# An MLP up-projection whose last low part is summed in SBUF by an adding GpSimd DMA

## The reference

```
def sq_relu_mlp(h, w_up, w_down):
    return jnp.square(jax.nn.relu(h @ w_up)) @ w_down
...
x = x + sq_relu_mlp(rms_norm(x, mlp_norm_g[l]), w_up[l], w_down[l])
```

## Time and profile before

| what | value |
|---|---|
| median of 2 runs | 2017.7 us (2017.51 to 2017.88) |
| profiled execution | span 2017.5 us, equal to the lower of the runs' times |
| TensorE busy | 2008.2 us, clock 0.999 of full |
| VectorE, ScalarE, GpSimd busy | 1520.8, 980.1, 13.2 us |
| DMA moved | 381.98 MB, 189 GB/s in the mean |
| a load of 1 MB, issue to landing | 5.0 to 5.3 us in the median |

### The profile page before, as it was taken

One profiled execution on the slowest core, in us unless ns is written; L12 is line 12 of the kernel. 1 busy time (PEld: TensorE's weight loads), 2 busy tenths in 40 slices (PEclk: granted clock), 3 DMA queues, 4 the chain that ended last, 5 costly groups with the idle time before them and its releaser, 6 DMA issues.

```text
span 2017.5 us, 26213 instructions
## 1 busy us (share of the span) xinstructions
PE 2008.2 (100%) x9284; PEld 1680.1 (83%) x9284; DVE 1520.8 (75%) x2217; ACT 980.1 (49%) x1263; POOL 13.2 (1%) x21
## 2 busy tenths in 40 slices
PE   9999999999999999999999999999999999999998
PEld 7888888888888888888888998888888888888887
DVE  7789998887568558757888787888558757855875
ACT  6555555444344434434446665554444434444443
POOL 0000000000000000000000000000000000000000
PEclk9999999999999999999999999999999999999999
DMA  8655555655555655655565554565655555565563
GB/s 297 214 170 189 181 167 176 209 194 193 193 190 179 209 189 185 208 189 185 188 208 172 139 150 146 198 219 188 208 188 187 204 191 187 175 218 188 168 219 114
DMA packets 218034, 381.98 MB, mean 189 GB/s; under 512 B 15600, under 2 KB 40560, under 8 KB 217968
## 3 DMA queue, kind: packets, MB, share of 16 engines
q1 hardware_dynamic: 217104, 379.03, 56.9%
q10 hardware_dynamic: 864, 2.10, 0.3%
HBM read 379.00 MB, written 2.10 MB: 189 GB/s over the span
## 4 chain that ended last, share of the span: by engine, by line
PE 97%; issue 2%; DVE 0%; ACT 0%; POOL 0%; POOLq 0%; DVEq 0%; ACTq 0%
PE acc L473 29%; PE acc L475 29%; PE acc L474 29%; PE acc L493 2%; PE acc L494 2%; PE acc L495 2%; PE acc L749 1%; PE acc L750 1%; PE acc L751 1%; PE side L802 0%; PE side L792 0%; PE side L560 0%; DVE wlo L1365 0%; PE side L571 0%; PE side L775 0%
## 5 line engine op out<-in xcount | busy, mean ns | idle before, releaser
L1365 DVE TENSOR_TENSOR wlo<-raw,whi 128x1024 fp32r<-128x1024 f32 (+2 forms) x700 | 836.2, 1212 | 357.2 <-ACT whi L896 353.8
L896 ACT ACTIVATE whi<-raw 128x1024 fp32r<-128x1024 f32 (+2 forms) x700 | 726.3, 1050 | 708.2 <-PE acc L475 677.1
L473 PE MATMUL acc<-whi,opB 128*128 128x512 f32 x1296 | 505.5, 390 | 0.0
L475 PE MATMUL acc<-whi,opB 128*128 128x512 f32 x1296 | 504.4, 389 | 0.0
L474 PE MATMUL acc<-wlo,opB 128*128 128x512 f32 x1296 | 504.2, 389 | 0.0
L473 PE MATMUL acc<-whi,opA 128*128 128x512 f32 (+2 forms) x1296 | 501.8, 387 | 0.0
L475 PE MATMUL acc<-whi,opA 128*128 128x512 f32 (+2 forms) x1296 | 501.0, 387 | 0.0
L474 PE MATMUL acc<-wlo,opA 128*128 128x512 f32 (+2 forms) x1296 | 501.0, 387 | 0.0
L475 PEld LDWEIGHTS acc<-whi,opB 128*128 128x128 f32 x1296 | 243.2, 188 | 50.7
L473 PEld LDWEIGHTS acc<-whi,opB 128*128 128x128 f32 x1296 | 243.3, 188 | 50.4 <-DVE wlo L1365 0.3
L474 PEld LDWEIGHTS acc<-wlo,opB 128*128 128x128 f32 x1296 | 243.3, 188 | 50.1
(11 more groups left out here) (256 smaller groups left out, 1109.0 us busy)
## 6 DMA issues: line engine op xcount, KB each, us to landing
raw<-in_w_up SPq DMA_DIRECT2D x128, 1024.0 KB, 5.3
raw<-in_w_down SPq DMA_DIRECT2D x128, 1024.0 KB, 5.0
raw<-in_a_w_qkv SPq DMA_DIRECT2D x44, 1024.0 KB, 5.1
raw<-in_a_w_o SPq DMA_DIRECT2D x16, 1024.0 KB, 5.0
raw<-in_b_w_o SPq DMA_DIRECT2D x16, 1024.0 KB, 5.0
raw<-in_w_ukv SPq DMA_DIRECT2D x32, 256.0 KB, 4.3
raw<-in_w_dkv SPq DMA_DIRECT2D x4, 1024.0 KB, 5.1
raw<-in_b_w_dq SPq DMA_DIRECT2D x4, 768.0 KB, 4.7
```

Source lines behind the costliest of these rows:

```text
L473: mm(o, a_hi, w_hi, start=first and c == 0, stop=False)
L475: done = mm(o, a_lo, w_hi, start=False, stop=last and c == chunks - 1)
L896: done = fn(whi[:, place:place + ch, 0:n], raw[:, r, c0:c0 + ch, 0:n], ACT.Copy)
L1365: done = tt_(wlo[:, place:place + ch, 0:n], raw[:, r, c0:c0 + ch, 0:n], whi[:, place:place + ch, 0:n].bitcast(F32), ALU.subtract)
```

## The change

In the 32 up blocks, half 7's low part isn't computed by VectorE. ScalarE writes the high part as before and then the raw weights times -1, rounded to fp32r, into `wlo` (that is minus the high part). GpSimd then issues a DMA that reads the same 256 rows by 512 columns of `w_up` from HBM, 512 KB, for a second time and adds them to what stands in `wlo[:, 6:8, :]`. TensorE waits for this sum (`lo_summed`) before half 7. VectorE skips half 7 and counts it in advance with half 6; SP, which overwrites `raw`, waits for ScalarE's second copy (`neg_ready`) before quad 3 of the next block. For this, SP's loops over the quarters are written in another order of nesting, with the same loads in the same order.

```diff
@@ SP @@
-            def whole(b, w, col, row=0):
+            def whole(b, w, col, row=0, summed=None):
                 for r in range(4):
+                    if r == 3 and summed is not None:
+                        sp.wait_ge(neg_ready, summed)
                     quad(b, r, w[:, bass.ds(row + 4 * r, 4), bass.ds(col, NB)])
...
-                with sp.Fori(0, QUARTERS) as q:
+                def up(q, j):
+                    n = JB * QUARTERS * l + JB * q + j
+                    whole(B_MLP[l] + 2 * JB * q + j, W_UP[l], D * q + NB * j,
+                          summed=None if isinstance(n, int) and n == 0 else n)
+
+                def down(q):
                     with sp.Fori(0, JB) as j:
-                        whole(B_MLP[l] + 2 * JB * q + j, W_UP[l], D * q + NB * j)
+                        whole(B_MLP[l] + 2 * JB * q + JB + j, W_DOWN[l], NB * j, row=KC * q,
+                              summed=JB * QUARTERS * l + JB * q + JB)
...
@@ GpSimd @@
+            def up_lo(l):
+
+                for n in range(JB * QUARTERS):
+                    pool.wait_ge(neg_ready, JB * QUARTERS * l + n + 1)
+                    pool.dma_start(wlo[:, 6:8, :], W_UP[l][:, KC - 2:KC, NB * n:NB * n + NB],
+                                   accum_op=ALU.add).then_inc(lo_summed, 16)
+
             stream_scale(0)
             with pool.Fori(0, DA_PAIRS) as p:
                 sub_norm(p)
+            up_lo(0)
             stream_scale(2)
...
+            up_lo(1)
...
@@ TensorE @@
+                def lo_ready_last(n, also=None):
+                    def ready(hf):
+                        if also:
+                            also(hf)
+                        if hf == 7:
+                            pe.wait_ge(lo_summed, 16 * n + 16)
+                    return ready
...
@@ ScalarE, split @@
                 done.then_inc(hi_ready, 1)
+                if kind == "up" and hf == 7:
+                    fn(wlo[:, place:place + 2, :], raw[:, r, c0:c0 + 2, :], ACT.Copy, scale=-1.0).then_inc(neg_ready, 1)
...
@@ VectorE, split @@
                 c0, place = 2 * (hf % 2), 2 * (hf % 4)
+                if kind == "up" and hf == 7:
+                    return
                 dve.wait_ge(hi_ready, 8 * b + hf + 1)
...
-                done.then_inc(lo_ready, 1)
+                done.then_inc(lo_ready, 2 if kind == "up" and hf == 6 else 1)
```

More of the change, by code:

```diff
@@ L252, in trunk @@
         lo_ready = sem("lo_ready")
+        neg_ready = sem("neg_ready")
+        lo_summed = sem("lo_summed")
         pe_halves = sem("pe_halves")
@@ L371, in mlp @@
             def mlp(l):
-                with sp.Fori(0, QUARTERS) as q:
-                    with sp.Fori(0, JB) as j:
-                        whole(B_MLP[l] + 2 * JB * q + j, W_UP[l], D * q + NB * j)
+                def up(q, j):
[3 more added lines that the diff above has]
+                def down(q):
+                    with sp.Fori(0, JB) as j:
+                        whole(B_MLP[l] + 2 * JB * q + JB + j, W_DOWN[l], NB * j, row=KC * q,
+                              summed=JB * QUARTERS * l + JB * q + JB)
+                for j in range(JB):
+                    up(0, j)
+                with sp.Fori(0, QUARTERS - 1) as q:
+                    down(q)
                     with sp.Fori(0, JB) as j:
-                        whole(B_MLP[l] + 2 * JB * q + JB + j, W_DOWN[l], NB * j, row=KC * q)
+                        up(q + 1, j)
+                down(QUARTERS - 1)
             mlp(0)
@@ L684, in up @@
                         for k in range(2):
-                            block_tok(B_MLP[l] + 2 * JB * q + 2 * i + k, 1 - k, u[1 - k] + U_QUARTER * q + i, opA)
+                            block_tok(B_MLP[l] + 2 * JB * q + 2 * i + k, 1 - k, u[1 - k] + U_QUARTER * q + i, opA,
+                                      ready=lo_ready_last(JB * QUARTERS * l + JB * q + 2 * i + k))
+                def lo_ready_last(n, also=None):
[5 more added lines that the diff above has]
+                    return ready
                 def hidden_ready(q):
@@ L691, in mlp @@
                     s = (j + 1) % 2
-                    block_tok(B_MLP[l] + j, s, u[s] + j // 2, opA, ready=None if j else opA_ready(v_in))
+                    block_tok(B_MLP[l] + j, s, u[s] + j // 2, opA,
+                              ready=lo_ready_last(JB * QUARTERS * l + j, None if j else opA_ready(v_in)))
                 with pe.Fori(0, QUARTERS - 1) as q:
@@ L1160, in up @@
                     for j in range(JB):
-                        body(B_MLP[l] + 2 * JB * q + j, {6: lambda: hid_high(q, j - 1)} if j else first)
+                        body(B_MLP[l] + 2 * JB * q + j, {6: lambda: hid_high(q, j - 1)} if j else first,
+                             kind="up")
                         drain_up(q, j)
@@ L1800, in up @@
                     for j in range(JB):
-                        body(B_MLP[l] + 2 * JB * q + j, turned(q, j - 1) if j else first)
+                        body(B_MLP[l] + 2 * JB * q + j, turned(q, j - 1) if j else first, kind="up")
                         square_up(q, j)
```

## The result

The changed kernel takes 2250.3 us in the median (2249.2 to 2251.3, 2 runs) against 2017.7: 1.115 times as long, 95% interval 1.113 to 1.117, or 232.6 us more. The profiled execution has a span of 2247.1 us, 229.6 more than before.

What follows compares the result with a forecast made beforehand. TensorE bounds the kernel, busy 2008.2 of 2017.5 us. A transfer of 1.0 + 5.3 + 2.2 = 8.5 us exceeds windows of 4.0 us (26 blocks) and 6.0 us (6): +132 us, 2150 us; 8-in-10 range 2065 to 2280.

Steps and rivals of the forecast that it cites:

- The case that was given 0.60: Whole kernel: TensorE waits for the sum without a lasting clock fall, 2057 to 2230 us, likeliest 2150.
- the rival that was given 0.27: Whole kernel: adding is slow or TensorE's clock falls, either taking the time over 2230 us; chance 0.27.
- slow adding: In the adding DMA: the bytes take 9 us, the transfer 12.2 us, cost 250 us, time 2268 us.
- The windows: From the negated copy's end to half 7's start: 4.0 us in 26 up blocks, 6.0 us in 6.
- Term 1: GpSimd's issue of the adding DMA, hand-over from ScalarE included: 1.0 us, ends 0.4 and 3 us.
- Term 2: The adding DMA's bytes, taken as two passes like a 1 MB load: 5.3 us, ends 4.1 and 9.
- Term 3: Company: SP's loads running beside the adding DMA lengthen it by 2.2 us, between 1.4 and 3.4.
- L: The adding DMA's time from ScalarE's increment to the last byte's semaphore: 8.5 us in all up blocks.
- The clock: TensorE at half clock for one half block behind each long wait: 71 us over 26 blocks, 2221 us.
- the second rival: Whole kernel: slow adding or a fallen TensorE clock, about 2340 us together; chance 0.27 of over 2230 us.
- The fitting case: At half 7: the transfer fits its window, nothing is 2% slower, 2018 to 2057 us, likeliest 2040; chance 0.12.

Runs made afterwards that it cites:

- Experiment 8: The changed kernel with the sum in a buffer of its own and the negated copy made behind half 4's: 2019.3 us, ratio 1.0006 to the kernel before.
- experiment 4: The changed kernel with SP's load of quad 3 held back until the sum has landed: 2104.2 us, ratio 1.042 to the kernel before.
- experiment 2: The changed kernel with GpSimd's DMA as a plain copy, the addition left out: 2135.5 us, ratio 1.058 to the kernel before.
- experiment 6: The changed kernel with ScalarE's negated copy moved ahead of the hidden copy and half 7's high part: 2066.3 us, ratio 1.024 to the kernel before.
- experiments 3 and 5: Changed kernel each time: 3 with the DMA summing only 256 KB, VectorE doing the rest, 2064.6 us; 5 with plain copy and quad 3 held back, 2054.4 us.
- experiment 7: The changed kernel with the negated copy first and SP's quad 3 held back until the sum has landed: 2052.6 us, ratio 1.017 to the kernel before.

## Why the prediction was right where it was, and what it had too small

The direction and its mechanism were right: every up block waits for the sum, in two kinds, 26 long and 6 shorter, and each wait adds to the end, since no later block catches up (158.8 + 71.3 against 229.6 us). Experiment 8 shows that nothing else in the change costs anything that can be measured (ratio 1.0006): ScalarE's second copy, SP's new order of loops, the traffic of a second read. The time lay in the range, 100 us above the 2150 named as likeliest. The case that was given 0.60, a full clock and 2057 to 2230 us, did not come. What came is the rival that was given 0.27, over 2230 us, with its clock and without its slow adding. By the prediction's steps:

- *The windows*, 4.0 and 6.0 us forecast. The block shown has 4.2 us, and the adding DMA's issue, 0.3 us behind the negated copy, stands 3.6 to 4.1 us ahead of half 7 in the late blocks and 5.7 in the early ones. Right.
- *Term 1, issue, 1.0 us* with the hand-over in it: 0.3 + 1.2 us, half a us too small. *Term 2, the bytes, 5.3 us*: a plain copy with quad 3 held back lands in 4.8 us, its 0.7 of issue included, and adding makes that 6.2. That leaves 5.0 us behind the issue, which is the term's size, though 0.4 of it can be quad 2 in the late blocks. Terms 1 and 2 were 6.3 together and measure 0.3 + 6.2 = 6.5. Right as a sum. The argument for term 2, a second pass worth 1.2 us, is borne out only in size: adding costs 1.4 us in all without company, and 0.5 of that is GpSimd's issue.
- *Term 3, company, 2.2 us*: 2.3 us measured in the early blocks, 3.1 in the late ones (experiment 4, 3.0 over all). Here the sum was too small, and only for the 26 late blocks. The term priced quad 3 alone; the load at 944.4 in the earlier trace rows, quad 0, falls into the same transfer, and the prediction named it and gave it no cost. The landing from issue was to be 7.5 us and is 9.2.
- *L, 8.5 us for both kinds*: about 9.8 us in the late blocks and 8.6 in the early ones, counted from the negated copy's end. The text said that the same sum serves both; it holds for the early kind (wait 2.5 forecast, 2.6 measured), while the late blocks (4.5 forecast, 5.7 measured) have quad 2 and the following quad 0 about as well. That they have more transfers near them was in the earlier trace rows, and the sum did not use it. The two kinds land 1.2 us apart, and 0.4 apart when quads 3 and 0 are held back. Waits in all: 132 us forecast, 164 measured.
- *The clock* was kept out of the likeliest case and put into the second rival, at 71 us for 26 falls of 2.72 us each. The busy time grew by 71.3 us. That the rival's 71 was met is luck, two errors that cancel: 30 falls instead of 26, at 71.3 / 30 = 2.4 us instead of 2.72. What failed is the judgment that waits of 4.5 us would probably not do it: in experiment 2 half clock follows every one of the 11 waits of 3.3 to 4.2 us. The earlier trace rows had shown the clock down 3.7 us behind the last matmul, which was reason enough to count it. The Trainium skill (TensorE: Matmul & The Clock Gate, HAM oscillation) says that a kernel which stops for DMA in every tile pays the fall of the clock again each time. The trace agrees: 30 of 32 waits were followed by half clock.
- *The fitting case*: even held back and plain, the DMA takes 4.8 us from issue, more than the late window of 4.1. By the formula of the Trainium skill (DMA: Bandwidth & Descriptors, Anatomy of one DMA) 3.2 us is the estimate for 512 KB, and by it the change would have been free. The runs don't agree with it: the quickest kernel's median is 4.8 us for 512 KB from GpSimd, its quickest transfer 3.8.

So two steps failed: the clock, left out of the likeliest case, which cost 71 us, and the company term with one L for both kinds, which was 0.9 us too small in the 26 late blocks, where the waits came out 1.2 us longer and 31 us more in all. Added up from the profile, the result is 2017.5 + 158.8 + 71.3 us. The slow adding of that rival (9 us for the bytes alone) is not what happened.

What stays open: no run holds back quad 2 or quad 0 alone, so the late blocks' extra 1.2 us (0.4 of it left without quads 3 and 0) is shared out by the kinds of block and not by an experiment. And when the clock falls is not told by these runs beyond the counts below: the length of the wait alone doesn't decide it.

## What to carry to other kernels

A transfer that is issued only when a shared place comes free has as its time the distance from there to the use, and that distance has to be held against the landing time under the traffic of that very moment; look at what else the same event releases, since here the semaphore that started the DMA also started a 1 MB load. If the chain doesn't fit, a place of its own, an earlier start or holding back the other load each cost a few lines, while relieving an engine that nobody waits for brings nothing. And where TensorE is the bound, count a pause of several us twice: once as it is, and once more for the clock, which here cost 71 us on top of 159.

## What the runs showed of the hardware that was not expected

- A DMA that adds in flight, 512 KB from GpSimd: 1.2 us of issue against 0.7 for a copy, and 6.2 us to land against 4.8. Beside SP's 1 MB loads: 9.2 against 6.6.
- Quad 3 landed in 8.0 to 10.3 us in the 23 blocks where it was issued 0.4 to 0.6 us behind the adding DMA, and in 5.5 to 6.0 us in the 6 where it was issued 0.1 us ahead. These blocks also differ in quads 2 and 0, so what makes the difference is not shown.
- The clock fell behind short pauses too: behind 30 of 32 waits where they were 2.4 to 6.7 us, behind 11 of 32 where they were 0.2 to 3.3 us (experiment 4), behind 3 of 32 in experiment 6, those of 3.0, 4.2 and 3.2 us, and behind none where all were under 2 us (experiments 3 and 5). The length alone did not decide: in the changed kernel the clock fell behind an early wait of 2.4 us and not behind those of 2.6 and 2.8 in two others, and in experiment 7 behind waits of 2.2 and 2.4 us and not behind the one of 2.6. In experiment 2 it fell behind 16 of 32, among them all those of 3.3 to 4.2 us. In the early block shown above it was granted in full at the restart and fell about 1 us later.
